# Output projections with tokens on the partitions, and a new order in the first stage, in a two-layer decoder step

## What is computed

```python
for l in range(DEPTH):                                     # DEPTH = 2
    shift, scale, gate = split(silu(c) @ w_ada[l] + b_ada[l], 3)   # one vector of 2048 per sequence
    h = rmsnorm(x, g_pre[l]) * (1 + scale) + shift
    y = (mixer(h @ w_in) * silu(z)) @ w_out                # w_out is 2048 x 2048
    x = x + gate * rmsnorm(y, g_post[l])                   # rmsnorm over the 2048 features
```

## Time and profile before

| | |
|---|---|
| median of 3 runs | 2303.77 us (2299.25 to 2305.38) |
| profiled execution, its own time | 2305.27 us |
| its span, first to last instruction | 2303.7 us |
| TensorE products, busy | 2173.2 us (94%) |
| TensorE weight loads, busy | 1983.9 us (86%, beside the products) |
| DVE, ACT, POOL busy | 963.2, 687.9, 65.6 us |
| products of L780 | 3 x 4320 of 128x128 by 272 columns |
| DMA | 300.5 MB, mean 130 GB/s |

### The profile page before, as it was taken

How to read it: one execution, slowest core, us unless ns; L and a number is a source line. 1 busy time by engine, 2 the same in 40 slices (tenths; PEclk the granted TensorE clock), 3 DMA queues, 4 the chain that set the end, 5 groups by cost and what they waited for, 6 DMA issues and landing times.

```text
span 2303.7 us, 40853 instructions
## 1 busy us (share of the span) xinstructions
PE 2173.2 (94%) x17140; PEld 1983.9 (86%) x17140; DVE 963.2 (42%) x1410; ACT 687.9 (30%) x1124; POOL 65.6 (3%) x109
## 2 busy tenths in 40 slices
PE   4789999999999999987999999999999999989995
PEld 2479989999999877775999999989999999977995
DVE  3423645546464421138433434343434343351225
ACT  3223434435343321124222222222222221232222
POOL 1000000000000000000000000000000000000000
PEclk8889999999999999998999999999999999989998
DMA  8893222232212699962657667786577688829522
GB/s 312 328 325 89 75 77 74 57 93 56 77 56 74 192 299 295 295 167 86 103 77 107 78 112 73 97 74 109 77 111 75 111 70 107 85 89 314 169 73 78
DMA packets 345885, 300.51 MB, mean 130 GB/s; under 512 B 8577, under 2 KB 287353, under 8 KB 344489
## 3 DMA queue, kind: packets, MB, share of 16 engines
q1 hardware_dynamic: 335952, 247.87, 51.8%
q0 software_dynamic: 9504, 50.19, 6.0%
q10 hardware_dynamic: 290, 0.32, 0.0%
HBM read 274.86 MB, written 27.56 MB: 131 GB/s over the span
## 4 chain that ended last, share of the span: by engine, by line
PE 85%; DVE 5%; DMA 5%; issue 2%; ACT 2%; SPq 1%; DVEq 0%; ACTq 0%
PE PJ L780 66%; DMA raw<-in_w_in_mlstm 3%; PE MX L997 3%; DMA obuf<-in_w_ada 2%; PE MX L926 1%; PE MX L935 1%; PE MX L949 1%; PE PJ L801 1%; PE MX L1147 1%; ACT w_hi L1220 1%; PE MX L889 1%; PE MX L1090 1%; PE MX L1103 1%; DVE arena L1625 1%; DVE obuf L1954 1%
## 5 line engine op out<-in xcount | busy, mean ns | idle before, releaser
L780 PE MATMUL PJ<-h_hi,w_hi 128*128 128x272 f32 x4320 | 928.5, 296 | 25.4 <-DVE h_lo L1663 13.1
L780 PE MATMUL PJ<-h_lo,w_hi 128*128 128x272 f32 x4320 | 898.8, 290 | 3.1 <-issue 3.1
L780 PE MATMUL PJ<-h_hi,w_lo 128*128 128x272 f32 x4320 | 900.5, 290 | 0.0
L780 PEld LDWEIGHTS PJ<-h_hi,w_hi 128*128 128x128 f32 x4320 | 684.2, 190 | 106.6 <-issue 87.5
L780 PEld LDWEIGHTS PJ<-h_lo,w_hi 128*128 128x128 f32 x4320 | 686.5, 191 | 1.2 <-issue 1.2
L780 PEld LDWEIGHTS PJ<-h_hi,w_lo 128*128 128x128 f32 x4320 | 682.3, 191 | 2.1 <-issue 2.1
L1603 DVE TENSOR_TENSOR w_lo<-raw,w_hi 128x2048 fp32r<-128x2048 f32 x106 | 242.8, 2292 | 384.4 <-ACT w_hi L1220 384.2
L1220 ACT ACTIVATE w_hi<-raw 128x2048 fp32r<-128x2048 f32 x106 | 202.3, 1909 | 50.8 <-DMA raw<-in_w_in_mlstm 47.0
L1928 DVE COPY modT<-MX 128x36 f32 x16 | 3.1, 196 | 210.8 <-PE MX L1008 210.8
L1529 ACT ACTIVATE arena<-PJ 128x544 f32<-128x544 f32 x32 | 20.0, 625 | 224.8 <-PE PJ L780 224.8
L1906 DVE TENSOR_TENSOR w_lo<-raw,w_hi 128x2048 fp32r<-128x2048 f32 x30 | 68.7, 2292 | 36.2 <-ACT w_hi L1426 36.2
(11 more groups left out here) (335 smaller groups left out, 1815.2 us busy)
## 6 DMA issues: line engine op xcount, KB each, us to landing
arena<-in_w_ada SPq DMA_DIRECT2D x64, 1024.0 KB, 5.3
raw<-in_w_in_mlstm SPq DMA_DIRECT2D x64, 1024.0 KB, 15.8
raw<-in_w_in_attn SPq DMA_DIRECT2D x40, 1024.0 KB, 5.7
obuf<-in_w_ada SPq DMA_DIRECT2D x32, 1024.0 KB, 9.6
raw<-in_w_out_attn SPq DMA_DIRECT2D x16, 1024.0 KB, 7.9
raw<-in_w_out_mlstm SPq DMA_DIRECT2D x16, 1024.0 KB, 6.2
arena<-x_spill POOLq DMA_DIRECT2D x2, 4352.0 KB, 17.0
arena<-in_state_C POOLq DMA_DIRECT2D x8, 1024.0 KB, 20.5
```

What stands on the lines that cost most here:

```text
L780: last = mm(PJ[:, 2 * pair + f, 0:HT], w, h[:, k, HT * f:HT * f + HT], start=(k == 0 and n == 0), stop=(k == KT - 1 and n == 2))
```

## The change

**Output projections.** The stationary operand is now 128 tokens of h, the moving one 512 columns of weights. A unit is 4 k blocks of 512 output columns (runs of 2 KB), and serves the four token tiles in turn, each in a PSUM bank of its own: 4 x 4 x 3 = 48 products of 512 columns. Four units make a group of columns. The 32 sample tokens are left out of these products; `sample_product` multiplies them in plain fp32 with the unsplit weights, spread over four column groups, and `sample_sum` adds these. ACT squares with a running sum along the row (`out_square`), DVE multiplies by gate x `g_post`, which is now held as rows (`gate_rows`, `gp`, `gs`). At the end each tile has its own root, reciprocal and `residual`, with x in rows, read again from `x_prompt`. Layer 0: a second sum and `x_scale` on the rows, then 64 transposes (`turn_rows`) and `full` give h by blocks, between the products of the gate unit. Layer 1: rows are stored as they are.

**First stage.** Units are ordered QQQQVK; the weights of the first four come as pairs of 256 columns (runs of 1 KB) and are split in halves. The third `mod_copy` is moved ahead of `modulate_group(0)`, and the DVE's third `mod_empty` ahead of `scale_group(0)`. The copy of x to DRAM is gone.

**Other moves.** `split_out` is cut in pieces; `memory` step 8 of the last head and `normaliser_turn` go into units 0 and 1 of the second output projection.

```diff
-L0P = "VQQQQK"
-L0K = "ZZ" + L0P
+OWNER = dict(A="d", Z="d", O="d", Q="a", K="a", V="a", Y="y", G="a")
+L0P = "QQQQVK"
+L0K = "ZZVQQQQK"
...
-SEGS = dict(out0=[(0, 2, None), (2, 4, (0, 2 * D, 8)), (6, 8, (1, 0, 12))],
-            out1=[(0, 2, None), (2, 4, (1, 2 * D, 20)), (6, 8, None)])
+GROUP_AT = dict(out0={k: 6 + k for k in range(2, 14)}, out1={k: 18 + k for k in range(2, 6)})
...
+OW = offsets([("x", 4 * D), ("gp", D), ("gs", 512), ("ys", 512), ("xs", 512), ("jk", 512), ("sel", N_X)])
...
+            def load_pair(n):
+                for half in range(2):
+                    sp.dma_start(raw[half][:, :].rearrange("p (k n) -> p k n", k=KT // 2),
+                                 win0[:, KT // 2 * half:KT // 2 * (half + 1), 2 * P * n:2 * P * n + 2 * P])\
+                        .then_inc(w_in[half], 16)
...
-                    for e in range(2):
-                        load_entry("l0p", (None, 0), e)
+                    load_pair(0)
...
+            sp.wait_ge(lo_done, 2)
+            load_pair(1)
...
+                    sp.wait_ge(lo_done, UNIT0[ph] + u - 1)
+                    if u >= 2:
+                        sp.wait_ge(raw_used, 16 * l + u - 1)
+                    sp.dma_start(raw[s][:, :].rearrange("p (k n) -> p k n", k=4),
+                                 w[:, 4 * q:4 * q + 4, 512 * g:512 * g + 512]).then_inc(w_in[s], 16)
...
-            pool.wait_ge(a0_used, 29)
-            for i in range(2):
-                cut = slice(KT // 2 * T * i, KT // 2 * T * (i + 1))
-                pool.dma_start(x_spill[:, cut], xflat[:, cut]).then_inc(spill0[i], 16)
-            pool.wait_ge(spill0[1], 16)
...
+            def out_inputs(l):
+                pool.dma_start(sel, const[:, C_X:C_X + N_X]).then_inc(gp_in, 16)
+                pool.dma_start(gp, g_post[l:l + 1, :].broadcast_to([P, D])).then_inc(gp_in, 16)
+                for g in range(4):
+                    pool.dma_start(gs[32 * g:32 * g + 32, :],
+                                   g_post[l:l + 1, 512 * g:512 * g + 512].broadcast_to([32, 512])).then_inc(gp_in, 16)
+            out_inputs(0)
...
-            pool.dma_start(xflat, x_spill).then_inc(reloaded, 16)
-            pool.wait_ge(x_ready, KT)
-            pool.dma_start(x_spill, xflat).then_inc(spilled, 16)
-            pool.wait_ge(spilled, 16)
+            pool.dma_start(xr, x_prompt[0].rearrange("(t p) d -> p t d", p=P)).then_inc(reloaded, 16)
+            pool.wait_ge(x_ready, 4)
+            pool.dma_start(x_spill[:, 0:4 * D], area(OW, "x")).then_inc(spilled, 16)
...
+            def gate_rows(n):
+                g = n - (8 if n < 12 else 20)
+                pe.wait_ge(mod_copied, n + 1)
+                pe.wait_ge(bias_in, n * 16 + 16)
+                pe.wait_ge(mod_taken, n - 7)
+                pe.wait_ge(gp_in, 96 if n < 12 else 192)
+                rows = misc[0:MROWS + 1, 0:512]
+                for j in range(4):
+                    mm(MX[32 * j:32 * j + 32, 3, :], sel[0:MROWS + 1, X_GP:X_GP + TS], rows, start=True, stop=True)
+                mm(MX[32 * g:32 * g + 32, 1, :], sel[0:MROWS + 1, X_GS:X_GS + TS], rows, start=True, stop=True)\
+                    .then_inc(mod_turned, 1)
+            def sample_product(l, u):
+                ph, g, q = f"out{l}", u // 4, u % 4
+                s = slot_of(ph, u)
+                pe.wait_ge(w_in[s], landed_at(ph, it0, u))
+                if g == 0:
+                    pe.wait_ge(h_ready, (2 * l + 1) * KT + 4 * q + 4)
+                elif q == 0:
+                    pe.wait_ge(samp_copied, 4 * l + g)
+                for j in range(4):
+                    last = mm(MX[32 * j:32 * j + 32, 0, :], obuf[:, 4 * q + j, TP:T], raw[s][:, 512 * j:512 * j + 512],
+                              start=(q == 0), stop=(q == 3))
+                last.then_inc(raw_used, 1)
+            def sample_sum(l, g):
+                pe.wait_ge(samp_copied, 4 * l + g + 1)
+                pe.wait_ge(mod_taken, g + (8, 20)[l] - 6)
+                mm(MX[32 * g:32 * g + 32, 1, :], sel[:, X_ST:X_ST + TS], scp[:, :], start=True, stop=True)\
+                    .then_inc(ysum_made, 1)
+            def square_sum(col):
+                for j in range(4):
+                    last = mm(MX[32 * j:32 * j + 32, 0, col:col + 1], sel[:, X_ST:X_ST + TS],
+                              st[:, (16, 35)[col]:(17, 36)[col]], start=True, stop=True)
+                last.then_inc(sum_s, 1)
+            def out_unit(l, u, points):
+                ph, g, q = f"out{l}", u // 4, u % 4
+                s = slot_of(ph, u)
+                pe.wait_ge(lo_done, UNIT0[ph] + u + 1)
+                for t in range(4):
+                    if u == 0 and t % 2 == 0:
+                        pe.wait_ge(*freed_at(ph, it0, t // 2 - 2))
+                    if q == 0 and g:
+                        pe.wait_ge(y_yg, 16 * l + 4 * g - 3 + t)
+                    for i in range(4):
+                        k = 4 * q + i
+                        if g == 0 and t == 0:
+                            pe.wait_ge(h_ready, (2 * l + 1) * KT + k + 1)
+                        hi, lo = w_hi[s][:, 512 * i:512 * i + 512], w_lo[s][:, 512 * i:512 * i + 512]
+                        for n, (h, w) in enumerate(((h_hi, hi), (h_hi, lo), (h_lo, hi))):
+                            last = mm(PJ[:, bank_of(l, t), :], h[:, k, P * t:P * t + P], w,
+                                      start=(k == 0 and n == 0), stop=(k == KT - 1 and n == 2))
+                        if i == 3 and t == 3:
+                            last.then_inc(w_used, 1)
+                        elif i == 3 and q == 3:
+                            last.then_inc(y_made, 1)
+                        for f in points.get(4 * t + i, ()):
+                            f()
...
+                    if u + 1 < KT and (u or not l):
+                        points[5].append(lambda u=u: sample_product(l, u + 1))
+                    if q == 3:
+                        points[8].append(lambda g=g: sample_sum(l, g))
...
+            def turn_rows(k, t):
+                last = tr(MX[:, (k + 1) % 4, P * t:P * t + P],
+                          obuf[:, 4 * t + k // 4, P * (k % 4):P * (k % 4) + P], ident)
+                if t == 3:
+                    last.then_inc(t_done, 1)
...
+                if k + 4 < KT:
+                    turn_block(k + 4)
...
+            out_product(1, [], {0: [(11, lambda: memory((None, MH - 1), 8)), (11, lambda: sample_product(1, 0)),
+                                    (11, lambda: sample_product(1, 1))],
+                                1: [(11, normaliser_turn)],
+                                2: [(14, lambda: pe.wait_ge(nT_done, 1))]})
...
+            mod_copy(2)
             modulate_group(0)
-            mod_copy(2)
...
+                    if ph == "l0z" and e == size:
+                        act.wait_ge(w_used, ended(ph, it, e - 1))
+                        act.wait_ge(om_done, 1 + OM * GR)
+                        act.wait_ge(zg_done, 2)
+                        split_out(range(4))
...
+            def out_square(l, g, t):
+                act.wait_ge(*tile_made(l, g, t))
+                act.wait_ge(y_sq, 16 * l + 4 * g + t)
+                act.wait_ge(ysq_s, 4 * l + g + (t > 1))
+                fn(jk, PJ[:, bank_of(l, t), :], ACT.Square, accum_out=st[:, 4 * t + g:4 * t + g + 1]).then_inc(y_sq, 1)
...
+            def x_square(t):
+                act.wait_ge(x_ready, t + 1)
+                fn(obuf[:, 4 * t:4 * t + 4, 0:512], xr[:, t, :].rearrange("p (a n) -> p a n", a=4), ACT.Square,
+                   accum_out=st[:, 31 + t:32 + t]).then_inc(x_sq, 1)
+                act.wait_ge(x_sq, t + 1)
+                fn(st[:, 36 + t:37 + t], st[:, 31 + t:32 + t], ACT.Sqrt, scale=1.0 / D, bias=st[:, 46:47])\
+                    .then_inc(srt_done, 1)
+            def x_scale(nth, t):
+                act.wait_ge(inv_done, nth)
+                fn(obuf[:, 4 * t + 2:4 * t + 4, 0:512], xr[:, t, 1024:2048].rearrange("p (a n) -> p a n", a=2),
+                   ACT.Copy, scale=st[:, 41 + t:42 + t]).then_inc(sc_a, 1)
...
+            def out_gated(l, g, t):
+                dve.wait_ge(y_sq, 16 * l + 4 * g + t + 1)
+                dve.wait_ge(mod_taken, g + (8, 20)[l] - 6)
+                tt(obuf[:, 4 * t + g, 0:512], PJ[:, bank_of(l, t), :], gp[:, 512 * g:512 * g + 512], ALU.mult)\
+                    .then_inc(y_yg, 1)
...
+            def residual(l, t, parts=1):
+                dve.wait_ge(reloaded, 16 * l + 16)
+                dve.wait_ge(y_yg, 16 * l + 13 + t)
+                n = 4 // parts
+                for i in range(parts):
+                    xt = xr[:, t, 512 * n * i:512 * n * i + 512 * n].rearrange("p (a n) -> p a n", a=n)
+                    stt(xt, obuf[:, 4 * t + n * i:4 * t + n * i + n, 0:512], st[:, 26 + t:27 + t], xt, ALU.mult, ALU.add)\
+                        .then_inc(x_ready, 1)
...
+            out_inverse(0, 1, 0)
+            residual(0, 0)
+            out_inverse(0, 2, 1)
```

(21 more changed lines are left out.)

683 lines of the change are left out of this document (403 added, 280 removed).

## The result

| | before | after | forecast |
|---|---|---|---|
| median | 2302.62 us (2299.25 to 2305.38, 4 runs) | 2289.46 us (2287.27 to 2291.67, 4 runs) | 2236 (2216 to 2262) |
| ratio | | 0.9948 (95%: 0.9932 to 0.9964) | 0.971 |
| profiled execution, span and its own time | 2303.7 and 2305.27 us | 2287.8 and 2289.4 us | |

The kernel is 0.5% faster, 13 to 16 us instead of 68, and 27 us above the range. Rows of the page after: busy time by engine, the clock in 40 slices, and the chain that ended last, by engine.

What follows compares the result with a forecast made beforehand. TensorE, busy 94% of the span, was taken as the bound. First projection +3.4, second -10.0, layer 0 to 1 -21.4, end -25.6, first stage -14: -67.6 from 2303.8 gives 2236 us; own range 2222 to 2250, stated range 2216 to 2262.

Steps and rivals of the forecast that it cites:

- the pace of 512 columns: Both output projections: 512-wide fp32r products start 0.217 us apart, bounds 0.2133 and 0.2357; 48 products of a unit take 10.42 us.
- the 12 ns: Excess of a 272-column product at full clock, 0.1252 against 0.1133 us; taken as a weight load that a longer stream covers.
- by the row with the same width: Basis for 0.217 us: a plain fp32 product of 512 columns, 0.86 us for four passes, read as 3.3 ns above 213.3 each.
- Time goes with columns: Rival in the output projections: a 512-wide product takes 0.236 us, 29 us more, 2265 in all; chance 0.12.
- list of what would make me wrong: Products 0.23 us or more apart, TensorE waiting for a bank, x back late, last DVE residual over 10 us after last product.
- layer 1 at nothing: Layer 1's eight heads, ahead of the second output projection: no term in the sum, so a forecast change of 0.
- the first stage: Start to the third unit: with the third copy first, that unit starts at 133 instead of 147.23; -14 us, bounds -18 and -3.
- Follow nearly without DMA waits: First stage, after the fourth group's turn at 83.9: eight `early` groups and 14 strips hardly wait; last turn ends at 123.7.
- the rival that the DMA feeds the chain: First stage keeps its end, as DMA or splitting feeds the chain: 3 us remain of 14, 2247 in all; chance 0.10.
- the three gaps of the second projection: TensorE's waits at the last head's passage to that projection, 3.6, 3.1 us and a smaller one: they go, one of 0.9 allowed.
- The middle: Layer 0 to layer 1: 42.7 us instead of 64.2, -21.4, bounds 36 and 50, as three of four token tiles are treated early.
- The end: Last product to the kernel's end: 10.6 us instead of 36.2, -25.6, bounds -28 and -21, without transposes.

## Why the prediction was wrong, and where it was right

**Wrong: the pace of 512 columns (23 of the 25.8 us of the projections).** The step was "the 12 ns look like a limit beside the stream, which a longer stream covers", and 0.217 taken "by the row with the same width", which was plain fp32. The rows show 0.2319: 1536 x 0.015 = 23 us. At full clock an fp32r product takes 7% more a column than 0.4167 ns, and 4 ns, in all 9% at 512; at half clock nothing more. My reading of the row was off as well: 0.86 us for four passes is 0.215 each, 1.7 ns above 213.3 and not 3.3. A full-clock row (272) against a half-clock row can't be split into columns and a fixed part, since the excess follows the columns. "Time goes with columns" (0.236, 2265 us) was the rival nearest to it, and got 0.12. Its condition stood in my list of what would make me wrong.

**Wrong: layer 1 at nothing (22.8 us).** The sum has no term for it, because the change doesn't touch its code. The prediction prices none of its loads, though the trace of the kernel before has a landing of 31.7 us at a need of one per 14.4, and 47.0 us of ACT waiting for them. The loss isn't that of one profile: layer 1 is 937 to 945 us in four profiles of the kernel before, 960 to 974 in ten of the changed one, and more than half of ACT's waits after lie in its first head. Two kernels that read the same columns at the same pace have different landing times, and each has nearly its own again in every execution. Declaring `const` first moves them; `w_in_mlstm` first, the widths tried, the size of the code and its shift don't. What in the changed program moves them against the kernel before stays open.

**Wrong in size: the first stage (-8.0, over all profiles -6.6, against -14).** The fourth group is turned at 82.73 (forecast 83.9), so the step before it was right. Behind it the chain does wait:

```profile
82.73 1.37 PE L831 MATMUL PJ<-fix,misc 106*128 106x9 f32 x8 [2.60 <-ACT misc L1409]
...
112.71 1.06 PE L820 MATMUL MX<-obuf,cT 128*32 128x512 f32 x8 [1.50 <-DMA obuf<-in_w_ada]
...
115.34 1.07 PE L820 MATMUL MX<-obuf,cT 128*32 128x512 f32 x8 [1.56 <-DMA obuf<-in_w_ada]
```

"Follow nearly without DMA waits" failed; the last turn is at 127.54 instead of 123.7, and half clock follows at 86 and behind a wait of 2.45 at 130.94. That the copy order carries the gain fell with the run that undid it: the rival that the DMA feeds the chain was the nearer one. What gives the 6.6 is not settled: the spill and the pairs were undone one at a time, the order of the Q, K and V units was not tried alone, nor all together.

**Wrong, small: the three gaps of the second projection.** I let two vanish; they are 1.12, 1.87 and 2.32, together 5.3 against 0.9. All three are waits for DVE: the second is for a block of h that it has not split yet, the third for the lower parts of a unit's weights. With the pace (768 x 0.015 = 11.5) they would be 15.9; the piece is 13.6 above forecast, as the 1.5 us allowed for half clock weren't needed (granted clock 1.00 from 2042 on). That leaves 0.8 us, which is open.

**Right.** The middle is 39.1 us (42.7 forecast, bounds 36 and 50). The end is 9.6 (10.6). In place of the 20 stores over 15.8 us of before, SyncE's timeline of after ends with these.

```profile
2271.43 9.47 SPq L638 DMA_DIRECT2D out<-arena  x6
...
2283.51 1.54 SPq L638 DMA_DIRECT2D out<-arena  x2
```

`sample_product` (1.2), `gate_rows` (2.04 against 2.05) and `sample_sum` (1.17 against 1.19) cost what the strips' rows gave. No group of a projection waits for its bank.

Together, from the profiled execution: 2305.3 - 67.6 = 2237.7; with the pace 2260.7; with the rest of the projections (2.8), the first stage (6.0), layer 0's heads (1.9) and the 4.7 gained 2266.7; with layer 1's 22.8 2289.5, as measured (2289.4). The range reached to 2262 and would have held the pace alone.

## What to carry to other kernels

Price a product from a row of its own type at the clock it will run at, and never split a fixed part out of rows at two clocks. Read the slowest landing, not the median, of every stream of loads that the change leaves alone, against the time for which it is issued ahead: a stream without slack can add a gain or a loss of its own to a change of the program. Before a change of 1% is credited, take the stalls out of both kernels (here 13 us became some 40), or run both with the tensors in another order (here 79).
